# Start addresses of the on-chip tiles: multiples of 256 bytes in place of 32, in a two-block float32 network

## What is computed

```
def swiglu(h, w_gate_up, w_down):
    g, u = jnp.split(h @ w_gate_up, 2, axis=-1)
    return (jax.nn.silu(g) * u) @ w_down

x = x + swiglu(rmsnorm(x, norm_ffn_g[layer]), ffn_w_gate_up[layer], ffn_w_down[layer])
...
x = x + 0.5 * _swiglu(_rmsnorm(x, ffn1_norm[i]), ffn1_w_gate[i], ffn1_w_up[i], ffn1_w_down[i])
```

## The kernel before

| tiles | start address | modulo 256 before |
|---|---|---|
| X, HH, HL, RAW, WH, WL, MEM, PAR | 16512 (X), 32896 (HH), 82048 (WH0), 98432 (WL0) | 128 |
| CON; ONES | 123456; 125792 | 64; 96 |
| T, SQ, RN | 126336 (T) | 128 |
| `low`: HIDH, HIDL, and all arenas that start there (OZ, XQ, XPT, HY, DQ, E1, DT, INV) | 134624 (HIDH), 179680 (HIDL) | 224 |
| SG, RS, SQB, ST, FEAT (counted from the top of memory) | 227296 (SG) | 224 |
| WF, FS, ZT, FWK, KR (over X and RAW to WL) | 16512 (WF) | 128 |

## Time and profile before

### The profile page before, as it was taken

The page is one execution under the profiler, slowest core; times in us unless marked ns, Lnnn a source line. Parts: engine busy times, 40 slices in busy tenths (PEclk is TensorE's granted clock), DMA queues, the critical chain, the costliest instruction groups (busy, mean ns, idle before and its releaser), DMA issues.

```text
span 3972.9 us, 41557 instructions
## 1 busy us (share of the span) xinstructions
PE 3749.9 (94%) x16918; PEld 3010.9 (76%) x16918; DVE 2039.7 (51%) x2512; ACT 1092.5 (28%) x1193; POOL 69.1 (2%) x81
## 2 busy tenths in 40 slices
PE   7999999979999999999998889999999998989997
PEld 5778888746778877888776678888888775868886
DVE  5565434463654435443765665434443656575442
ACT  2242222242432222222342222222222242322221
POOL 0000000000000000000010000000000102000000
PEclk9999999998999999999989999999999999999998
DMA  3222222110222222222312212222222313112221
GB/s 123 94 74 97 95 88 103 63 38 23 85 98 98 90 90 78 101 90 101 126 35 83 85 68 92 101 92 93 96 98 91 126 64 96 64 64 95 95 91 68
DMA packets 66783, 342.91 MB, mean 86 GB/s; under 512 B 23525, under 2 KB 23525, under 8 KB 30817
## 3 DMA queue, kind: packets, MB, share of 16 engines
q1 hardware_dynamic: 60864, 303.19, 21.8%
q0 software_dynamic: 5792, 37.92, 2.6%
HBM read 324.31 MB, written 16.78 MB: 86 GB/s over the span
## 4 chain that ended last, share of the span: by engine, by line
PE 87%; DVE 8%; ACT 2%; issue 1%; DMA 1%; SPq 0%; DVEq 0%; ACTq 0%
PE ACC L984 25%; PE ACC L986 25%; PE ACC L985 25%; PE ACC L1604 1%; PE ACC L1342 1%; DVE BX L2850 1%; DVE BT L2848 1%; PE ACC L1322 1%; PE MIX L1254 1%; DVE WL L2257 0%; DVE PT L3037 0%; DVE PT L3039 0%; DMA RAW<-wall 0%; DMA XIT<-blocks_out 0%; PE MIX L1151 0%
## 5 line engine op out<-in xcount | busy, mean ns | idle before, releaser
L984 PE MATMUL ACC<-HH,WH 128*128 128x512 f32 (+1 forms) x3322 | 1315.0, 396 | 72.9 <-DVE HL L2452 44.6
L985 PE MATMUL ACC<-HL,WH 128*128 128x512 f32 (+1 forms) x3322 | 1298.2, 391 | 0.0
L986 PE MATMUL ACC<-HH,WL 128*128 128x512 f32 (+1 forms) x3322 | 1297.9, 391 | 0.0
L2257 DVE TENSOR_TENSOR WL<-RAW,WH 128x2048 fp32r<-128x2048 f32 x292 | 668.4, 2289 | 495.8 <-ACT WH L1768 495.3
L984 PEld LDWEIGHTS ACC<-HH,WH 128*128 128x128 f32 x3322 | 631.8, 190 | 227.1 <-issue 80.1
L985 PEld LDWEIGHTS ACC<-HL,WH 128*128 128x128 f32 x3322 | 631.9, 190 | 132.6 <-issue 5.2
L986 PEld LDWEIGHTS ACC<-HH,WL 128*128 128x128 f32 x3322 | 631.5, 190 | 130.9
L1768 ACT ACTIVATE WH<-RAW 128x2048 fp32r<-128x2048 f32 x292 | 556.5, 1906 | 575.2 <-PE ACC L986 570.8
L986 PE MATMUL ACC<-HIDH,WL 128*128 128x512 f32 x1056 | 421.3, 399 | 0.0
L985 PE MATMUL ACC<-HIDL,WH 128*128 128x512 f32 x1056 | 416.1, 394 | 0.0
L984 PE MATMUL ACC<-HIDH,WH 128*128 128x512 f32 x1056 | 414.0, 392 | 0.0
(11 more groups left out here) (499 smaller groups left out, 2902.9 us busy)
## 6 DMA issues: line engine op xcount, KB each, us to landing
RAW<-wall SPq DMA_DIRECT2D x261, 1024.0 KB, 4.8
RAW<-wall SPq DMA_DIRECT2D x24, 768.0 KB, 4.1
KR<-spectra POOLq DMA_DIRECT2D x4, 2048.0 KB, 9.6
x_kept<-X POOLq DMA_DIRECT2D x2, 2048.0 KB, 6.9
FWK<-mats POOLq DMA_DIRECT2D x4, 1024.0 KB, 5.4
spectra<-SQ POOLq DMA_DIRECT2D x8, 512.0 KB, 3.0
spectra<-T POOLq DMA_DIRECT2D x8, 512.0 KB, 3.5
X<-x_kept POOLq DMA_DIRECT2D x2, 2048.0 KB, 14.9
```

The source lines that it names most:

```text
L984: pe.matmul(out_ap, wh, hh, start=first, stop=False)
L985: pe.matmul(out_ap, wh, hl, start=False, stop=False)
L986: return pe.matmul(out_ap, wl, hh, start=False, stop=last)
L2257: v.tensor_tensor(WL[n % 2][:], RAW[n % 2][:], WH[n % 2][:], ALU.subtract).then_inc(w_lo, 1)
```

## The change

The running top starts at a multiple of 256 (16640), and `low`, where the arenas begin, is rounded up to one (134912). Sizes are still rounded to 32, and the tiles placed from the top of memory stay where they are.

```
-        top = [(nc.sbuf_base + 31) // 32 * 32]
+        top = [(nc.sbuf_base + 255) // 256 * 256]
...
-        low = top[0]
+        low = (top[0] + 255) // 256 * 256
```

## The result

The changed kernel takes 3953.24 us at the median of 5 runs (3948.14 to 3954.41), against 3975.01 before (5 runs, 3972.07 to 3980.45): a ratio of 0.9943, with a 95% interval of 0.9931 to 0.9954. The forecast was 3954.0. The profiled execution has a span of 3946.3 us.

What follows compares the result with a forecast made beforehand. TensorE, busy 94% of the 3972.9 us span, was taken as the bound. Down-projections 21.1 plus transfers 0.2 gave 21.3 us off, a span of 3951.6; with 2.4 added for the median, 3954.0 us, range 3948 to 3960.

Steps and rivals of the forecast that it cites:

- Which matmuls, how many, and how much each: Down-projections: 3168 matmuls with HIDH on three lines, in six stages, each save 6.67 ns, 21.1 us in all.
- What would be late next: Down-projections: load 4.8 us, ACT 1.9, DVE 2.3 stay hidden behind 48 matmuls per weight unit, 10.9 us.
- The up-projections and the rest of the three-part matmuls: Matmuls with HH or WH moving go from 128 to 0 modulo 256; taken as 0 gain.
- The large gain: All full-rate matmuls: the fixed 12 ns is also a misaligned start and goes; some 184 us off, 3791; chance 0.10.
- VectorE and DMA: Vector edits cost nothing, under 1 us either way; loads show no sign of address, transfers 0.2 us, bounds 0 to 1.5.
- The 0.2 us that the sum has for transfers: First load and short transfers around the solve, on the chain: 0.2 us saved, bounds 0 to 1.5.
- the extra transaction: DMA: a transfer beginning off a multiple of 256 bytes pays one more, an estimated 4 beats in 256 on 8 KB rows.
- The mechanism: Moving rows of 2048 bytes: HH covers 32 blocks of 64 bytes, HIDH touches 33; one block more is 16 columns, 6.67 ns.
- blocks of 64: Moving rows are taken in 64-byte pieces; a row starting inside one touches 33 instead of 32, costing 16 columns more.
- no change: Down-projections: HIDH is slow for another reason, lying above byte 131072 or its distance from WH; 3975 us; chance 0.17.
- Slower: HH matmuls: a start in the first half of a 256-byte line is bad, HH pays 6.67 ns; 4044 us; chance 0.07.
- The chance of 0.60: Whole kernel: probability given to the forecast's own case, 3954.0 us, range 3948 to 3960.

Runs made afterwards that it cites:

- the weights off: Against the kernel before, RAW, WH, WL and all tiles behind them moved up by 32 bytes, HH staying: 4028.35 us, ratio 1.0128.
- `low` alone: Against the kernel before, only `low` rounded up to a multiple of 256, the running top left as it was: 3973.65 us, ratio 0.9996.

## Why the prediction was right, and where it was wrong

*Which matmuls, how many, and how much each.* Right: 3168 matmuls of the down-projections, 6.67 ns each, 21.1 us foretold and 21.2 measured, 3.5 us in each of six stages. That came from two steps compared at equal shape, type and clock, and needed no mechanism. What would be late next (the load, ACT and VectorE) was not, as worked out.

*The up-projections and the rest of the three-part matmuls.* Right at nothing: 226.7 ns before and after. The large gain is refuted: with all operands at multiples of 256 the 13 ns over 512 columns are still there. The sum took this part as fixed for each instruction, whatever the address. For 512 columns no run went below 226.7, but for 256 columns it isn't fixed: of the 13 ns over 106.7 some 3 go at distance 32 (the weights off). What the rest is was not tried. That plain matmuls take two passes is a reading of their 430 ns, twice 215; no row shows the passes one by one. (The smallest of the means in the earlier trace rows is 392, not 391; nothing rests on it.)

*VectorE and DMA.* Right. L2589 and L3065 have medians of 692 and 691 ns, loads of 1 MB into FWK and INV land in 5.5 and 5.3 us, and the first load on the chain is 12.33 us against 12.62. These are within what one execution scatters. The 0.2 us that the sum has for transfers is shown by no run, and the extra transaction that the prediction cites can't be seen in these loads.

*The mechanism.* Wrong. The step that failed is "A row of HH covers 32 blocks exactly; a row of HIDH begins in the middle of one", drawn from two addresses and a difference of 16 columns. It gave the right time because, in the full change, distance 0 and alignment to 64 come together. It would have given 3954 for `low` alone too, which brings HIDH to a multiple of 64, and that measured 3973.65. So the right time was in part luck: the price was read rightly from two rows, but that it would go rested on the wrong cause. The agreement with 16 columns was no proof: with 8 columns left out the step was again 544 or 560 columns' time, and not where blocks of 64 put it.

*The rivals.* The sentence "or its distance from WH matters" stood among the reasons for no change. That was the true cause, put in the wrong case: the table of addresses shows that the change takes the distance from 352 to 0, because the top moves by 128 and `low` by 288. Had I worked that out, this reason would have stood on the side of the gain. "Slower" as put (a start in the first half of a line being bad) is refuted by the 226.7 ns after. The chance of 0.60 was for a time whose mechanism no third address confirmed, and the coincidence of two mechanisms carried it.

*What stays open.* That HIDH at 128 modulo 512, with the weights at 128, is as fast as after the change follows from the table, but this kernel was not run. Nor was a distance of 256 with all rows at it: whether the starts must agree modulo 512 or only modulo 256 is open. Nor was one of 32, the cheapest for 256 columns. Why distance matters is argued only as follows, and why mixed distances can cost less not at all. In the trace a weight load starts with each matmul and runs beside it, here in the changed kernel:

```profile
541.15 0.39 PE L986 MATMUL ACC<-HIDH,WL 128*128 128x512 f32 x1
541.15 0.19 PEld L984 LDWEIGHTS ACC<-HIDH,WH 128*128 128x128 f32 x1
541.38 0.39 PE L984 MATMUL ACC<-HIDH,WH 128*128 128x512 f32 x1
541.38 0.19 PEld L985 LDWEIGHTS ACC<-HIDL,WH 128*128 128x128 f32 x1
```

So two streams are read from the same memory at the same time, and how far apart they run may decide whether they meet. No run takes away one of the streams, so this is a guess. The Trainium skill ("SBUF — State Buffer", Who interferes with whom) gives TensorE two independent read ports and has it wait on no one. The table above has 233.3 and 226.7 ns for the same instructions, a cost by address that this rule doesn't have; whether the ports are where it comes from, no run shows.

## What to carry to other kernels

Compare the start-to-start steps of equal matmuls in different stages; a difference of a few per cent between operands in different tiles is real time, and moving a tile is cheap to try. For fp32r matmuls of 512 columns, place the tiles so that the moving rows and the stationary slices have the same start modulo 512, and measure again where the shape is another one; a round number for each of them is not what counts, and a group moved without its partner can cost more than the right place gains (1.3% against 0.6% here). When two edits of a change each do nothing alone, look for a quantity that only both together set.

## What the runs showed of the hardware that I had not expected

- The step of an fp32r matmul of 512 columns at 2.4 GHz is 226.7, 233.3 or 234.3 ns by the distance between its two operands' addresses, at otherwise equal instructions; with the distance mixed, 229 was seen. At granted clock 0.50 it is 426.7 ns at distances 0 and 480 alike.
- With 256 columns the step is 119.8 ns at distance 0, 116.8 at 32 and 119.9 at 96.
- The step is the same whether VectorE, ScalarE and GpSimd work or idle beside it (233.38 and 233.33 ns before, 226.67 both after).
- Neither half of the placement change has an effect (0.9995 and 0.9996), both have 0.9943.
- Leaving out 8 of 512 columns took 6.7 ns off the step in one place and nothing in the other.
